# A hybrid encoder layer on one core: the embedding's squares are taken during the first gate pieces of the last stage instead of ahead of and during the down projection

## The chip, the core and the metric

The kernel runs on one core of a Trainium2 chip. A core has a matrix engine (TensorE, PE in the profile), a vector engine (VectorE, DVE), a scalar engine (ScalarE, ACT), GpSimd (POOL) and a queue that issues DMAs (SP). Each runs its own list of instructions in order; they meet at semaphores. The metric is the device time of one execution in microseconds (us), the median of several.

## The reference, cut to what matters

```python
def rmsnorm(x, g):
    y = x32 * lax.rsqrt(jnp.mean(x32 * x32, axis=-1, keepdims=True) + RMS_EPS)
    return (y * g.astype(jnp.float32)).astype(x.dtype)
...
    gu = rmsnorm(h, g_ffn[i]) @ w_gate_up[i]
    g_, u_ = gu[..., :D_FF], gu[..., D_FF:]
    h = h + (jax.nn.silu(g_) * u_) @ w_down[i]

    e = rmsnorm(p[i] @ w_ple_proj[i], g_ple_post[i])
    gate = jax.nn.sigmoid(rmsnorm(h, g_ple[i]) @ w_ple_gate[i])
    h = h + gate * e
return rmsnorm(h, g_final)
```

There are 512 tokens and 2048 model columns. Ahead of these lines come the two attention branches, which the change doesn't touch. Two norms matter here. The **residual's norm** is that of `h` after the down projection: the gate's matmul takes `h` unnormed and its result is scaled by the norm afterwards. The **embedding's norm** is that of `p @ w_ple_proj`, called `e` before it is normed.

## The kernel before, in words

Everything is held transposed: 128 columns of the model on the partitions, 512 tokens along a row, so `h` (`res`) and `e` (`emb`) are 16 tiles of 128x512 each. Float32 products are made exact by splitting each operand in a high and a low part. A **piece** of weights is 512x256: SP loads it to `raw`, ACT copies the high part (`whi`, L726, `w_hi<-raw`), DVE subtracts it for the low part (`wlo`, L1165, `w_lo<-raw,w_hi`), and PE does 24 matmuls with it (4 row tiles, 2 column tiles, 3 products: L375 to L377). There are two buffers of split weights, so ACT's split of piece n+2 waits until PE has finished piece n.

The end of the program has these stages. **E** (4 pieces, E0 to E3): the embedding's projection; DVE copies each finished pair of tiles to `emb`. **D** (8 pieces, D0 to D7): the last down projection. For each d, DVE adds the product of D<d> to the residual (`add_residual`, L1496), ACT copies the high part of the two new residual tiles times their gain (L726, `r<-res,gn`), and DVE computes their low parts (`gain_lo`, L1200). **G** (32 pieces, G0 to G31): the gate's matmul, eight groups of four pieces. The code calls the pieces `N_E + j`, `N_D + d` and `N_PLE + j`; a group of G is `g` there. The last group, with the final norm's tail, is cut in halves of the tokens.

A norm needs a sum of squares over 16 tiles. ACT squares a tile into one of two slots of `tab` (`square`, L744), POOL adds the slot to a running sum (`add_square`, L1633 for the first, a copy, and L1636 for the others), and each square waits until the slot's last sum is done. PE adds over the partitions with a matrix of ones (`total`, L399), ACT takes a logarithm and an exponential (`root`, L749 and L752), and DVE refines the result (`recip`, four instructions, L1184 to L1191). In code, `total(5, 3)` and `root(4, ...)` with `recip(4, ...)` are the residual's norm, `total(4, 2)` and `root(5, ...)` with `recip(5, ...)` the embedding's.

Before the change ACT takes the embedding's squares three at a time from E1 on (`three_squares`), 16 of the embedding, then 16 of the residual, until D's last piece. So at d = 2 to 7 the squares of residual tiles come in threes or twos, some an iteration late; at d = 6 and d = 7 two squares of new tiles stand between the residual's add and the copies with gain. Both norms are finished during G4 to G7.

In stage G, for each group, DVE scales PE's result (`empty`, L1177), ACT takes a sigmoid (L1127), DVE norms two embedding tiles (L1583, `emb<-emb,gn,rstd`), POOL multiplies the two (L1665) and adds the result to the residual (L1673), and ACT squares the new residual for the final norm and copies it with its gain (`after_gate`). The order of each engine's list is written out by hand.

Of the kernel before, what the change touches and what calls it, by code (L numbers as in the profile page):

```python
# [95 lines left out]
def build(nc, xT, pT, gains, tables, mats, w_in, w_qb, w_kvb, w_a, w_b, w_o, w_gu, w_dn, w_pg, w_pp, outT):  # L96
    with ExitStack() as ctx:
# [77 lines left out]
        def ff_pair(g):  # L175
            return (g - G_FF + 2) % 4
# [193 lines left out]
        def _(pe):  # L370
# [24 lines left out]

            def total(norm, bank):

                pe.wait_ge(acc_done, [16, 20, 24, 40, 56, 72][norm])
                mm(ps[:, bank, :], ones, sums(norm), start=True, stop=True).then_inc(tot_done, 1)  # L399

            def head_total(m):
# [229 lines left out]
            def n_group(g, n, pair):  # L631
                free(g, 4)
                for j in range(4):
                    piece(n + j, j, 2 * pair, [n_tile(4 * j + k) for k in range(4)], j == 0, j == 3)
# [45 lines left out]
                piece(N_PLE + j, j, 2 * ff_pair(G_PLE), [n_tile(4 * j + k) for k in range(4)], j == 0, j == 3)  # L680
            pe.wait_ge(emptied, G_PLE)
            total(5, 3)
            total(4, 2)
            n_group(G_PLE + 1, N_PLE + 4, ff_pair(G_PLE + 1))
            n_group(G_PLE + 2, N_PLE + 8, ff_pair(G_PLE + 2))
            pe.wait_ge(rstd_done, 6)
            n_group(G_PLE + 3, N_PLE + 12, ff_pair(G_PLE + 3))
# [36 lines left out]
        def _(act):  # L724
# [15 lines left out]
            def square(s, tile, sq, need, count):  # L740
                act.wait_ge(need, count)
                if s >= 2:
                    act.wait_ge(acc_done, s - 1)
                nc.scalar.activation(sq[:, s % 2, :], tile, ACT.Square).then_inc(sq_done, 1)  # L744
# [315 lines left out]
            def chunk(c, last):  # L1060


                b, g = c * 24 + N_FF_LOOP, c * 12 + G_FF
                four(b)
                whi(b + 6, 2)
                ff_hidden(c * 2, 0, b)
                for j in range(3):
                    whi(b + 7 + j, (3 + j) % 4)
                ff_gate(g + 2)
                four(b + 8)  # L1070
                if not last:
                    whi(b + 14, 2)
                    ff_hidden(c * 2 + 1, 1, b)
                    for j in range(3):
                        whi(b + 15 + j, (3 + j) % 4)
                    ff_gate(g + 4)
                    for d in range(8):
                        whi(b + 18 + d, (2 + d) % 4)
                else:
                    for i in range(4):  # L1080
                        whi(b + 14 + i, (2 + i) % 4)
                        if i == 0:
                            ff_hidden(c * 2 + 1, 1, b)
                        if i:
                            three_squares(i - 1)

            def three_squares(slot):

                for i in range(3 * slot, min(3 * slot + 3, 32)):
                    k, g = i % 16, (G_E if i < 16 else G_D) + i % 16 // 2  # L1090
                    square(40 + i, emb[:, k, :] if i < 16 else res[:, k, :], sq_b, emptied, g + 1)

            with act.Fori(0, CHUNKS - 1) as c:
                chunk(c, False)
# [1 line left out]
            ln_exp_table()  # L1096
            for d in range(8):
                whi(N_D + d + 2, (2 + d) % 4)
                three_squares(3 + d)
                for t in range(2):  # L1100
                    k = 2 * d + t
                    act.wait_ge(emptied, G_D + d + 1)
                    copy(n_tile(k)[:, 0, :], res[:, k, :], gn[:, G_PLEN + k:G_PLEN + k + 1]).then_inc(u_hi, 1)
# [4 lines left out]
                for k in (2 * g, 2 * g + 1):  # L1108
                    copy(emb[:, k, :], res[:, k, :], gn[:, G_FIN + k:G_FIN + k + 1]).then_inc(gained, 1)

            for g in range(8):
                b = N_PLE + 4 * g
                if g not in (1, 7):
                    whi(b + 2, 2)
                if g < 7:
                    whi(b + 3, 3)
                if g:
                    after_gate(g - 1)
                for j in range(0 if g == 7 else 4 if g == 6 else 2):
                    whi(b + 4 + j, j)  # L1120
                if g == 0:
                    root(4, 3, 2, D)
                    root(5, 2, 1, D)
                    whi(b + 6, 2)
                if g < 7:
                    act.wait_ge(emptied, G_PLE + g + 1)
                    nc.scalar.activation(tmp[:, 0:2, :], tmp[:, 0:2, :], ACT.Sigmoid).then_inc(pg_sig, 1)  # L1127
            def tail_sigmoid(th, t):
                act.wait_ge(tail_emptied, 2 * th + t + 1)
                x = tmp[:, t, HALF[th]]  # L1130
# [21 lines left out]
        def _(dve):  # L1152
# [40 lines left out]
            def recip(turn, norm, bank, r, width, t=slice(0, SEQ)):  # L1193
                refined(rstd[:, r, t], sums(norm)[:, t], ps[:, bank, t], width, log_done, root_done, turn, refine,
                        rstd_done)
                dve.wait_ge(rstd_done, turn + 1)
# [367 lines left out]
            for d in range(8):  # L1564
# [2 lines left out]
                dve.wait_ge(emptied, G_D + d + 1)  # L1567
                for k in (2 * d, 2 * d + 1):
                    gain_lo(n_tile(k), res[:, k, :], G_PLEN + k, 42 + k)
            for g in range(8):  # L1570
                for j in range(1 if g == 1 else 0, 0 if g == 7 else 6 if g == 6 else 4):
                    wlo(N_PLE + 4 * g + 2 + j, (2 + j) % 4)
                if g == 0:
                    recip(4, 5, 3, 2, D)
                if g:
                    dve.wait_ge(pg_res, g)
                if g < 7:
                    empty(tmp[:, 0:2, :], 2 * ff_pair(G_PLE + g), 2, N_PLE + 4 * g + 3)
                if g == 0:
                    wlo(N_PLE + 6, 2)  # L1580
                    recip(5, 4, 2, 1, D)
                for k in (2 * g, 2 * g + 1):
                    stt(emb[:, k, :], emb[:, k, :], gn[:, G_POST + k:G_POST + k + 1], rstd[:, 1, :],  # L1583
                        ALU.mult, ALU.mult).then_inc(emb_normed, 1)

            def tail_empty(th, t):
                dve.wait_ge(tail_tile, 2 * th + t + 1)
# [34 lines left out]
        @block.gpsimd  # L1622
        def _(pool):
            def add_square(s, first, norm, sq):

                out = sums(norm)
                pool.wait_ge(sq_done, s + 1)
                if s == first:
                    if norm == 4:
                        pool.wait_ge(u_lo, 42)  # L1630
                    elif norm:
                        pool.wait_ge(rstd_done, 4 if norm == 5 else norm)
                    nc.gpsimd.tensor_copy(out, sq[:, s % 2, :]).then_inc(acc_done, 1)  # L1633
                else:
                    pool.wait_ge(acc_done, s)
                    nc.gpsimd.tensor_tensor(out, out, sq[:, s % 2, :], ALU.add).then_inc(acc_done, 1)  # L1636

            sq_a, sq_b = tmp[:, 2:4, :], tab[:, 0:2, :]
            for norm, first, end in ((0, 0, 16), (1, 16, 20), (2, 20, 24)):
                for s in range(first, end):  # L1640
                    add_square(s, first, norm, sq_a)

            for p in range(8):
                pool.wait_ge(emptied, G_MERGE + p + 1)
                if p:
                    pool.wait_ge(mrg_lo, p)
                else:
                    pool.wait_ge(gated_a_out[0], 16 * HEADS // 2)
                nc.gpsimd.tensor_tensor(tmp[:, 0:2, :], tmp[:, 2:4, :],  # L1649
                                        res[:, GATE_IN[p % 2]:GATE_IN[p % 2] + 2, :], ALU.add).then_inc(mrg_sum, 1)  # L1650
            for s in range(24, 40):
                add_square(s, 24, 3, sq_b)
            with pool.Fori(0, CHUNKS) as c:
                for half in range(2):
                    pool.wait_ge(emptied, c * 12 + G_FF + 2 + 2 * half)
                    pool.wait_ge(ff_act, c * 2 + half + 1)
                    nc.gpsimd.tensor_tensor(tmp[:, 2:4, :], tmp[:, 2:4, :], tmp[:, 0:2, :],  # L1657
                                            ALU.mult).then_inc(ff_mul, 1)
            for norm, first in ((4, 40), (5, 56)):
                for s in range(first, first + 16):  # L1660
                    add_square(s, first, norm, sq_b)
            for g in range(7):
                pool.wait_ge(pg_sig, g + 1)
                pool.wait_ge(emb_normed, 2 * g + 2)
                nc.gpsimd.tensor_tensor(tmp[:, 0:2, :], tmp[:, 0:2, :], emb[:, 2 * g:2 * g + 2, :],  # L1665
                                        ALU.mult).then_inc(pg_mul, 1)
                pool.wait_ge(pg_mul, g + 1)
                if g == 0:
                    pool.wait_ge(u_hi, 58)
                    pool.wait_ge(u_lo, 58)  # L1670
                    pool.wait_ge(sq_done, 72)
                r = res[:, 2 * g:2 * g + 2, :]
                nc.gpsimd.tensor_tensor(r, r, tmp[:, 0:2, :], ALU.add).then_inc(pg_res, 1)  # L1673
                for s in (72 + 2 * g, 73 + 2 * g):
                    add_square(s, 72, 6, sq_b)
# [77 lines left out]
```

## Time and profile before

| what | us |
|---|---|
| median of 3 runs | 2825.78 (2824.82 to 2825.94) |
| the profiled execution's own time | 2825.82 |
| its span, first to last instruction | 2824.0 |
| PE busy | 2793.9 of 2824.0 |
| DVE, ACT, POOL busy | 1216.2, 886.5, 236.2 |
| PE waiting for DVE's low parts (L1165), whole program | 5.0, six times |

The span is 1.8 us shorter than the execution's own time; a shift of the program's end moves both alike. PE is busy in 99% of the span, so little else can matter: the other engines count only where PE waits for them, and those places are few and short.

### The profile page before, as it was taken

Reading aid. Unit: us, or ns where it says so; the run is one execution under the profiler, and the core shown is the slowest. Engines: PE = TensorE matmul, PEld = TensorE weight load, DVE = VectorE, ACT = ScalarE, POOL = GpSimd, SP = SyncE. Lnnn points to the kernel's source line nnn. Section 1 sums busy time; section 2 is a strip of 40 time slices with the busy share of each in tenths; the row PEclk is TensorE's granted clock in tenths of the full one; section 3 lists DMA queues with packets and bytes.
Section 4 is the critical chain, followed back from the end, with each engine's and each line's share of the span. In section 5 each row is a group of like instructions: output and inputs, shape, how many; then the busy total and the mean of one; then the engine's idle time right before and its main releaser. Section 6 shows DMA issues by size and latency. Waiting matters only on the chain.

```text
span 2824.0 us, 32043 instructions
## 1 busy us (share of the span) xinstructions
PE 2793.9 (99%) x12532; PEld 2305.4 (82%) x12532; DVE 1216.2 (43%) x1268; ACT 886.5 (31%) x1105; POOL 236.2 (8%) x134
## 2 busy tenths in 40 slices
PE   8999999999999999999999999999999999999998
PEld 6878888888888888888888888888888888888787
DVE  5455545455664434433333333334333333335535
ACT  5234334334554233322222222222222222224433
POOL 3000000010000211000000000000000000004332
PEclk9999999999999999999999999999999999999999
DMA  6333333333224643333333333333333333333232
GB/s 197 96 90 105 102 99 104 97 90 112 94 94 140 206 144 97 99 103 97 97 97 97 97 97 97 96 96 96 97 95 96 95 96 96 96 97 94 90 97 97
DMA packets 278895, 295.20 MB, mean 105 GB/s; under 512 B 9008, under 2 KB 261040, under 8 KB 278704
## 3 DMA queue, kind: packets, MB, share of 16 engines
q1 hardware_dynamic: 274336, 285.90, 32.6%
q10 hardware_dynamic: 4496, 8.44, 0.8%
q8 instruction: 42, 0.69, 0.1%
q14 instruction: 21, 0.17, 0.0%
HBM read 277.53 MB, written 16.78 MB: 104 GB/s over the span
## 4 chain that ended last, share of the span: by engine, by line
PE 94%; DVE 2%; POOL 2%; ACT 1%; issue 1%; DMA 0%; DVEq 0%; POOLq 0%; ACTq 0%
PE ps L375 31%; PE ps L377 31%; PE ps L376 31%; PE ps L441 1%; POOL acc L1636 1%; POOL tab L1636 1%; DVE w_lo L1165 1%; PE ps L430 0%; DVE r L1200 0%; ACT r L726 0%; PE ps L403 0%; ACT w_hi L726 0%; ACT tab L744 0%; DVE emb L1603 0%; PE ps L399 0%
## 5 line engine op out<-in xcount | busy, mean ns | idle before, releaser
L375 PE MATMUL ps<-r,w_hi 128*128 128x512 f32 x3840 | 1505.7, 392 | 13.1 <-DVE r L1200 8.1
L377 PE MATMUL ps<-r,w_lo 128*128 128x512 f32 x3840 | 1496.1, 390 | 0.0
L376 PE MATMUL ps<-r,w_hi 128*128 128x512 f32 x3840 | 1495.8, 390 | 0.0
L1165 DVE TENSOR_TENSOR w_lo<-raw,w_hi 128x1024 fp32r<-128x1024 f32 x484 | 612.1, 1265 | 1409.8 <-ACT w_hi L726 1409.0
L726 ACT ACTIVATE w_hi<-raw 128x1024 fp32r<-128x1024 f32 x484 | 512.7, 1059 | 1543.6 <-PE ps L377 1534.9
L375 PEld LDWEIGHTS ps<-r,w_hi 128*128 128x128 f32 x3840 | 721.9, 188 | 172.0 <-issue 13.0
L376 PEld LDWEIGHTS ps<-r,w_hi 128*128 128x128 f32 x3840 | 721.9, 188 | 151.7 <-issue 3.4
L377 PEld LDWEIGHTS ps<-r,w_lo 128*128 128x128 f32 x3840 | 721.7, 188 | 150.7
L1657 POOL TENSOR_TENSOR tmp<-tmp 128x1024 f32<-128x1024 f32 x22 | 52.6, 2392 | 1339.0 <-DVE tmp L1177 1339.0
L1496 DVE TENSOR_TENSOR res<-ps,res 128x1024 f32<-128x1024 f32 x96 | 116.8, 1216 | 0.0
L1177 DVE TENSOR_TENSOR tmp<-ps,rstd 128x1024 f32<-128x1024 f32 x69 | 83.9, 1217 | 1.6 <-PE ps L377 1.5
L1636 POOL TENSOR_TENSOR acc<-acc,tab 128x512 f32<-128x512 f32 x43 | 66.2, 1540 | 157.0 <-ACT tab L744 153.6
L726 ACT ACTIVATE r<-ps 128x512 fp32r<-128x512 f32 (+1 forms) x98 | 53.9, 594 | 58.9 <-PE ps L377 48.5
L375 PE MATMUL ps<-r 128*128 128x512 f32 (+1 forms) x192 | 69.6, 363 | 1.3 <-DVE r L1226 1.3
L377 PE MATMUL ps<-r 128*128 128x512 f32 (+1 forms) x192 | 68.1, 355 | 0.0
L376 PE MATMUL ps<-r 128*128 128x512 f32 (+1 forms) x192 | 68.0, 354 | 0.0
L1200 DVE SCALAR_TENSOR_TENSOR r<-res,gn,r 128x512 fp32r<-128x512 f32 x48 | 48.3, 1040 | 21.9 <-ACT r L726 21.9
L1649 POOL TENSOR_TENSOR tmp<-tmp,res 128x1024 f32<-128x1024 f32 x8 | 20.0, 2505 | 350.0 <-DVE tmp L1418 350.0
L1633 POOL COPY acc<-tmp 128x512 f32<-128x512 f32 x3 | 2.0, 683 | 546.0 <-ACT tmp L744 546.0
L1247 DVE TENSOR_TENSOR r<-ps,r 128x512 fp32r<-128x512 f32 x64 | 41.0, 681 | 7.5 <-ACT r L726 7.5
L726 ACT ACTIVATE r<-res 128x512 fp32r<-128x512 f32 (+1 forms) x39 | 24.6, 630 | 62.1 <-DVE res L1219 52.8
L726 ACT ACTIVATE r<-tmp 128x1024 fp32r<-128x1024 f32 x30 | 31.5, 1049 | 38.9 <-POOL tmp L1649 38.1
(104 smaller groups left out, 969.8 us busy)
## 6 DMA issues: line engine op xcount, KB each, us to landing
raw<-w_gu SPq DMA_DIRECT2D x176, 512.0 KB, 3.6
raw<-w_in SPq DMA_DIRECT2D x108, 512.0 KB, 3.7
raw<-w_dn SPq DMA_DIRECT2D x88, 512.0 KB, 3.4
raw<-w_o SPq DMA_DIRECT2D x32, 512.0 KB, 3.4
raw<-w_pg SPq DMA_DIRECT2D x32, 512.0 KB, 3.4
gates<-tmp ACTq DMA_DIRECT2D x16, 512.0 KB, 2.8
raw<-w_a SPq DMA_DIRECT2D x16, 512.0 KB, 3.7
res<-gates SPq DMA_DIRECT2D x16, 512.0 KB, 5.3
```

Of the source, the lines that this page charges most:

```text
L375: mm(out, hi, x[:, 0, :], start=start, stop=False)
L376: mm(out, hi, x[:, 1, :], start=False, stop=False)
L377: return mm(out, lo, x[:, 0, :], start=False, stop=stop)
L441: i = nc.tensor.transpose(ps[:, banks[kt], q * P:(q + 1) * P], res[:, PROB + q, kt * P:(kt + 1) * P], ident)
L726: return nc.scalar.activation(out, in_, ACT.Copy, scale=scale)
L1165: tt(w_lo[:, j % HL], raw[:, j], w_hi[:, j % HL], ALU.subtract).then_inc(w_lo_done, 1)
L1177: tt(out, ps[:, bank:bank + 2, :], both(r), ALU.mult).then_inc(emptied, 1)
L1200: stt(out[:, 1, :], in_, gn[:, gain:gain + 1], out[:, 0, :], ALU.mult, ALU.subtract).then_inc(u_lo, 1)
L1247: tt(pt[kt % 3][:, 1, :], ps[:, banks[kt], :], pt[kt % 3][:, 0, :], ALU.subtract).then_inc(pt_lo, 1)
L1496: tt(r, ps[:, 2 * pair:2 * pair + 2, :], r, ALU.add).then_inc(emptied, 1)
L1636: nc.gpsimd.tensor_tensor(out, out, sq[:, s % 2, :], ALU.add).then_inc(acc_done, 1)
L1657: nc.gpsimd.tensor_tensor(tmp[:, 2:4, :], tmp[:, 2:4, :], tmp[:, 0:2, :], ALU.mult).then_inc(ff_mul, 1)
```

## The change

Three things move. The squares of the residual keep their place in D, but are alone there: two for each d, right after the residual's add and ahead of the two copies with gain. The squares of the embedding go to stage G: three after the split of G2, of G3 and of G4, three more after G6's, four after G7's. And the embedding's norm follows one group later: PE's total stands after G7 instead of ahead of G4, ACT's root after the split of G9, DVE's refinement after G9's low part, and DVE norms the embedding tiles of groups 0 and 1 together there.

```diff
-                pe.wait_ge(acc_done, [16, 20, 24, 40, 56, 72][norm])
+                pe.wait_ge(acc_done, [16, 20, 24, 40, 72, 56][norm])
...
             total(5, 3)
+            n_group(G_PLE + 1, N_PLE + 4, ff_pair(G_PLE + 1))
             total(4, 2)
-            n_group(G_PLE + 1, N_PLE + 4, ff_pair(G_PLE + 1))
...
-                        if i:
-                            three_squares(i - 1)
-
-            def three_squares(slot):
-
-                for i in range(3 * slot, min(3 * slot + 3, 32)):
-                    k, g = i % 16, (G_E if i < 16 else G_D) + i % 16 // 2
-                    square(40 + i, emb[:, k, :] if i < 16 else res[:, k, :], sq_b, emptied, g + 1)
+
+            def emb_squares(k0, k1):
+
+                for k in range(k0, k1):
+                    square(56 + k, emb[:, k, :], sq_b, emptied, G_D)
...
                 whi(N_D + d + 2, (2 + d) % 4)
-                three_squares(3 + d)
+                for t in range(2):
+                    k = 2 * d + t
+                    square(40 + k, res[:, k, :], sq_b, emptied, G_D + d + 1)
...
+            for i in range(3):
+                whi(N_PLE + 2 + i, (2 + i) % 4)
+                emb_squares(3 * i, 3 * i + 3)
+            whi(N_PLE + 5, 1)
+            root(4, 3, 2, D)
+            whi(N_PLE + 6, 2)
+            ple_sigmoid(0)
+            emb_squares(9, 12)
+            whi(N_PLE + 7, 3)
+            emb_squares(12, 16)
+            whi(N_PLE + 8, 0)
+            whi(N_PLE + 9, 1)
+            root(5, 2, 1, D)
+            whi(N_PLE + 10, 2)
+            whi(N_PLE + 11, 3)
+            after_gate(0)
+            ple_sigmoid(1)
+            whi(N_PLE + 12, 0)
+            after_gate(1)
+            whi(N_PLE + 13, 1)
+            ple_sigmoid(2)
...
+            for j in range(2, 6):
+                wlo(N_PLE + j, j % 4)
+            recip(4, 5, 3, 2, D)
+            ple_empty(0)
+            for j in range(6, 10):
+                wlo(N_PLE + j, j % 4)
+            recip(5, 4, 2, 1, D)
+            emb_norm(0)
+            emb_norm(1)
+            wlo(N_PLE + 10, 2)
+            wlo(N_PLE + 11, 3)
+            ple_empty(1)
+            emb_norm(2)
+            wlo(N_PLE + 12, 0)
+            wlo(N_PLE + 13, 1)
+            ple_empty(2)
...
-            for norm, first in ((4, 40), (5, 56)):
+            for norm, first in ((5, 40), (4, 56)):
```

Line numbers shift by up to 17 in the changed kernel; the helpers are the same. The first place is ACT's list in stage D, from the split of D3 to that of D5 (`tab<-emb` and `tab<-res` are squares, `r<-res,gn` the copies with gain). Before:

```order
L726 ACTIVATE w_hi<-raw 128x1024
L744 ACTIVATE tab<-emb 128x512 x3
L726 ACTIVATE r<-res,gn 128x512 x2
L726 ACTIVATE w_hi<-raw 128x1024
L744 ACTIVATE tab<-emb 128x512
L744 ACTIVATE tab<-res 128x512 x2
L726 ACTIVATE r<-res,gn 128x512 x2
L726 ACTIVATE w_hi<-raw 128x1024
```

The same stretch in the changed kernel:

```order
L726 ACTIVATE w_hi<-raw 128x1024
L744 ACTIVATE tab<-res 128x512 x2
L726 ACTIVATE r<-res,gn 128x512 x2
L726 ACTIVATE w_hi<-raw 128x1024
L744 ACTIVATE tab<-res 128x512 x2
L726 ACTIVATE r<-res,gn 128x512 x2
L726 ACTIVATE w_hi<-raw 128x1024
```

The embedding's squares are gone, and in every iteration two squares of the tiles that the copies read next stand ahead of those copies.

The second place is ACT's list from the split of G7 to that of G11, in the changed kernel. L749 and L752 are the logarithm and the exponential of the embedding's norm; before, they stood right behind the residual's, ahead of the split of G6, with no table load between or ahead of them.

```order
L726 ACTIVATE w_hi<-raw 128x1024
L744 ACTIVATE tab<-emb 128x512 x4
L726 ACTIVATE w_hi<-raw 128x1024 x2
L749 ACT_TABLE_LOAD
L749 ACTIVATE rstd<-ps,eps 128x512
L752 ACT_TABLE_LOAD
L752 ACTIVATE rstd<-rstd 128x512
L726 ACTIVATE w_hi<-raw 128x1024 x2
```

The first sigmoid now stands ahead of this root, so two loads of ACT's function tables come with it, and a third ahead of the next sigmoid.

The third place is DVE's list from the four subtractions of G6 to G9 to those of G10 and G11, in the changed kernel (L1201 to L1208 are `recip`, L1594 the embedding's norm):

```order
L1182 TENSOR_TENSOR w_lo<-raw,w_hi 128x1024 x4
L1201 TENSOR_SCALAR tab<-ps 128x512
L1204 TENSOR_TENSOR tab<-tab,rstd 128x512
L1206 SCALAR_TENSOR_TENSOR tab<-tab,rstd 128x512
L1208 SCALAR_TENSOR_TENSOR rstd<-tab,rstd 128x512
L1594 SCALAR_TENSOR_TENSOR emb<-emb,gn,rstd 128x512 x4
L1182 TENSOR_TENSOR w_lo<-raw,w_hi 128x1024 x2
```

Before, `recip` of the embedding stood after the subtraction of G6 with two `emb` instructions behind it, and three subtractions behind those. Now it stands after G9's, with four `emb` instructions between it and G10's subtraction.

## Rows read from the trace of the kernel before

**Rows 1.** The page's first part: busy us, share of the span, instructions.

```profile
PE 2793.9 (99%) x12532; PEld 2305.4 (82%) x12532; DVE 1216.2 (43%) x1268; ACT 886.5 (31%) x1105; POOL 236.2 (8%) x134
```

**Rows 2.** Waits of PE, whole program: total us, times, longest.

```profile
PE ps L375 <- DVE w_lo L1165: 5.0, 6, 1.1
```

**Rows 3.** Timeline of PE, its late starts: start us, us, what, [idle, releaser].

```profile
2614.07 0.47 PE L375 MATMUL ps<-r,w_hi 128*128 128x512 f32 x1 [0.56 <-DVE w_lo L1165]
...
2639.55 0.47 PE L375 MATMUL ps<-r,w_hi 128*128 128x512 f32 x1 [0.90 <-DVE w_lo L1165]
...
2675.22 0.47 PE L375 MATMUL ps<-r,w_hi 128*128 128x512 f32 x1 [1.02 <-DVE w_lo L1165]
```

**Rows 4.** Timeline of ACT: splits of E2, D2, G4, G5, G6, G10.

```profile
2564.64 1.06 ACT L726 ACTIVATE w_hi<-raw 128x1024 fp32r<-128x1024 f32 x1 [4.38 <-PE ps L377]
...
2586.48 1.06 ACT L726 ACTIVATE w_hi<-raw 128x1024 fp32r<-128x1024 f32 x1
...
2645.34 1.06 ACT L726 ACTIVATE w_hi<-raw 128x1024 fp32r<-128x1024 f32 x1 [5.54 <-PE ps L377]
2650.78 1.06 ACT L726 ACTIVATE w_hi<-raw 128x1024 fp32r<-128x1024 f32 x1 [4.38 <-PE ps L377]
...
2657.98 1.06 ACT L726 ACTIVATE w_hi<-raw 128x1024 fp32r<-128x1024 f32 x1 [3.67 <-PE ps L377]
...
2681.04 1.06 ACT L726 ACTIVATE w_hi<-raw 128x1024 fp32r<-128x1024 f32 x1 [2.20 <-PE ps L377]
```

**Rows 5.** Timeline, iteration d = 7 of stage D: DVE, then ACT.

```profile
2631.56 1.21 DVE L1165 TENSOR_TENSOR w_lo<-raw,w_hi 128x1024 fp32r<-128x1024 f32 x1
2632.70 1.21 DVE L1496 TENSOR_TENSOR res<-ps,res 128x1024 f32<-128x1024 f32 x1
2635.81 2.45 DVE L1200 SCALAR_TENSOR_TENSOR r<-res,gn,r 128x512 fp32r<-128x512 f32 x2 [1.90 <-ACT r L726]
2638.19 1.21 DVE L1165 TENSOR_TENSOR w_lo<-raw,w_hi 128x1024 fp32r<-128x1024 f32 x1
...
2633.94 1.15 ACT L744 ACTIVATE tab<-res 128x512 f32<-128x512 f32 x2 [3.29 <-DVE res L1496]
2635.00 1.32 ACT L726 ACTIVATE r<-res,gn 128x512 fp32r<-128x512 f32 x2
```

**Rows 6.** Timeline of POOL and DVE where they overlap.

```profile
2609.90 1.78 DVE L1200 SCALAR_TENSOR_TENSOR r<-res,gn,r 128x512 fp32r<-128x512 f32 x1
2611.29 1.55 POOL L1636 TENSOR_TENSOR acc<-acc,tab 128x512 f32<-128x512 f32 x1
2611.61 2.31 DVE L1165 TENSOR_TENSOR w_lo<-raw,w_hi 128x1024 fp32r<-128x1024 f32 x1
...
2681.68 2.40 POOL L1673 TENSOR_TENSOR res<-res,tmp 128x1024 f32<-128x1024 f32 x1
2682.14 3.03 DVE L1165 TENSOR_TENSOR w_lo<-raw,w_hi 128x1024 fp32r<-128x1024 f32 x1 [3.06 <-ACT w_hi L726]
...
2636.09 1.62 POOL L1636 TENSOR_TENSOR acc<-acc,tab 128x512 f32<-128x512 f32 x1
2636.48 1.78 DVE L1200 SCALAR_TENSOR_TENSOR r<-res,gn,r 128x512 fp32r<-128x512 f32 x1
...
2602.13 0.61 POOL L1633 COPY acc<-tab 128x512 f32<-128x512 f32 x1
```

**Rows 7.** Timeline: ACT's table load and a root; DVE's recip and norm.

```profile
2585.18 1.28 ACT L797 ACT_TABLE_LOAD   x1
...
2651.74 0.67 ACT L749 ACTIVATE rstd<-ps,eps 128x512 f32<-128x512 f32 x1
2652.44 0.63 ACT L752 ACTIVATE rstd<-rstd 128x512 f32<-128x512 f32 x1
...
2661.01 0.69 DVE L1187 TENSOR_TENSOR tab<-tab,rstd 128x512 f32<-128x512 f32 x1
...
2663.18 1.42 DVE L1583 SCALAR_TENSOR_TENSOR emb<-emb,gn,rstd 128x512 f32<-128x512 f32 x2
```

More of the change, by code:

```diff
@@ L1109, in after_gate, with ple_sigmoid @@
                     copy(emb[:, k, :], res[:, k, :], gn[:, G_FIN + k:G_FIN + k + 1]).then_inc(gained, 1)
-            for g in range(8):
+            def ple_sigmoid(g):
+                act.wait_ge(emptied, G_PLE + g + 1)
+                nc.scalar.activation(tmp[:, 0:2, :], tmp[:, 0:2, :], ACT.Sigmoid).then_inc(pg_sig, 1)
+            for i in range(3):
[19 more added lines that the diff above has]
+            ple_sigmoid(2)
+            for g in range(3, 8):
                 b = N_PLE + 4 * g
-                if g not in (1, 7):
+                if g < 7:
                     whi(b + 2, 2)
-                if g < 7:
                     whi(b + 3, 3)
-                if g:
-                    after_gate(g - 1)
+                after_gate(g - 1)
                 for j in range(0 if g == 7 else 4 if g == 6 else 2):
                     whi(b + 4 + j, j)
[L1121 to L1124, printed above, removed]
                 if g < 7:
-                    act.wait_ge(emptied, G_PLE + g + 1)
-                    nc.scalar.activation(tmp[:, 0:2, :], tmp[:, 0:2, :], ACT.Sigmoid).then_inc(pg_sig, 1)
+                    ple_sigmoid(g)
             def tail_sigmoid(th, t):
@@ L1569, in _, with ple_empty, emb_norm @@
                     gain_lo(n_tile(k), res[:, k, :], G_PLEN + k, 42 + k)
[L1570 to L1574, printed above, removed]
+            def ple_empty(g):
                 if g:
                     dve.wait_ge(pg_res, g)
[L1577 to L1581, printed above, removed]
+                empty(tmp[:, 0:2, :], 2 * ff_pair(G_PLE + g), 2, N_PLE + 4 * g + 3)
+            def emb_norm(g):
                 for k in (2 * g, 2 * g + 1):
@@ L1584, in _ @@
                         ALU.mult, ALU.mult).then_inc(emb_normed, 1)
+            for j in range(2, 6):
[14 more added lines that the diff above has]
+            ple_empty(2)
+            for g in range(3, 8):
+                for j in range(0 if g == 7 else 6 if g == 6 else 4):
+                    wlo(N_PLE + 4 * g + 2 + j, (2 + j) % 4)
+                if g < 7:
+                    ple_empty(g)
+                else:
+                    dve.wait_ge(pg_res, 7)
+                emb_norm(g)
             def tail_empty(th, t):
```

## The prediction

> **What bounds the kernel now.** I read the page's busy shares first: PE works 99% of the span [rows 1], so a change of the other engines is worth only what it does to PE's waits. The list of PE's waits comes next: the one that repeats is for DVE's low parts, six times, 5.0 us [rows 2]. PE's timeline then says where: five late starts are in this part of the program, four between D6 and G2 (the first and the last are shown) and one at G8 [rows 3].
>
> An idle time of PE is not the whole loss, so I count in finishing times. ACT's split of piece n+2 waits for PE's end of piece n, and where ACT was idle its start is that end. Undisturbed pieces end 5.44 us apart (2645.34 to 2650.78) and the two totals together cost 2657.98 - 2650.78 - 5.44 = 1.76, so 0.88 each [rows 4]. E0 ends at 2564.64, so D0 ends four pieces later at 2586.40; ten more give 2640.80 for G2, and the row has 2645.34: stage D and the first gate pieces lose **4.54 us** [rows 4]. G7 then ends at 2645.34 + 5 x 5.44 + 1.76 = 2674.30, G8 should at 2679.74 and does at 2681.04: **1.30 us** [rows 4]. After that nothing is late until the tail. A late low part makes its piece end 5.95 us after it: G2's ends at 2638.19 + 1.21 = 2639.40, G2 itself at 2645.34 [rows 4, 5].
>
> Why is stage D late? One iteration shows it [rows 5]. DVE's chain is: subtraction at 2631.56, add at 2632.70, then it waits for ACT, which after the add makes two squares (2633.94) and only then the copies (2635.00); the two `gain_lo` start at 2635.81, the next subtraction at 2638.19. That is 6.63 us a piece against PE's 5.44. Part of the 6.63 is the second `gain_lo`, 1.78 long.
>
> **DVE and POOL exclude each other.** POOL's add started at 2611.29 while a `gain_lo` ran, DVE's next subtraction was issued at 2611.61, and they ended in the order gain, add (2612.84), subtraction (2613.92): the waiting POOL instruction went in between two DVE instructions, and the subtraction took 2.31 us for 1.21, ending 1.08 after the add. Behind a 2.40 us add on POOL a subtraction took 3.03, ending 1.09 after it; a `gain_lo` ended at 2638.26, 0.55 after the add that held it [rows 6]. DVE instructions that read a bank of sums (`res<-ps,res`) keep their 1.21 next to POOL [rows 5]. So POOL's work on 1024 elements, 2.4 us, blocks a whole low part. The Trainium skill ("SBUF — State Buffer", Who interferes with whom) has this as an exclusive lock for DVE instructions with two inputs in SBUF; by that, the trace agrees, and it speaks against putting DVE's embedding norm just ahead of a needed subtraction.
>
> **The change part by part.**
>
> Stage E: ACT loses its squares and POOL its adds. PE wasn't late there, so 0. D2's split starts at 2586.40 and not 2586.48, where a table load had held it [rows 4, 7], its subtraction at 2587.49.
>
> Stage D: the loop now has at every d the form that d = 7 had: two squares of new tiles, then the copies. I take the measured 6.63 for each, since the same instructions stand in the same order with POOL idle at the start [rows 5]. The first iteration I estimate at 6.38: there POOL's first instruction is a copy of 0.61 [rows 6] in place of an add, and by my stepping through it DVE is held 0.25 less. So G2's subtraction is issued at 2587.49 + 6.38 + 7 x 6.63 = 2640.28. Before it was 2638.19: the seven iterations from D2's subtraction (2586.48 + 1.09) to 2631.56 took 6.28 on average [rows 4, 5], less than 6.63, since most had squares of tiles that were long ready and could be made before the add. I add one collision: the first embedding square's copy on POOL is ready about 2640.0, while the last `gain_lo` runs (to 2640.35), gets in ahead of the subtraction and takes 0.47. The subtraction ends at 2640.35 + 0.47 + 1.08 = 2641.90 (2641.5 without the collision, 2643 if it were an add), G2 at 2647.85: **+2.51 us** against before.
>
> G3 to G8: one total stays ahead of G4, so G7 ends at 2647.85 + 27.20 + 0.88 = 2675.93. ACT's 16 embedding squares go at POOL's pace, an add each of 1.3 us alone and up to 1.2 more behind a DVE instruction (1.55 and 1.62 in [rows 6] after short waits). Their tightest place is behind G7's split: four squares put G8's split at about 2672.1, and its subtraction, behind POOL's last add, ends at 2675.5. With the second total ahead of G8, PE needs it by 2676.3, so G8 is in time by 0.8 and the old wait there is gone: **-1.30 us**. That wait had come from `after_gate(0)` ahead of G8's split, and this now stands behind G11's.
>
> G10: here a new wait forms. From G7's end (t = 0): split of G9 1.06; table load 1.28; logarithm 0.67; second load 1.28; exponential 0.63; with 0.02 between them the root is done at 5.00 [rows 7]. DVE's remaining three of `recip` take from their start to the first norm instruction 2663.18 - 2661.01 = 2.17 [rows 7], with 0.11 to notice: 7.28. The norm instructions follow every 0.67 [rows 7]. After two of them (8.70) POOL may start its first product, gets in after the third (9.37) and ends at 11.62 (2.40 less the 0.15 of overlap that a waiting POOL instruction shows); the fourth norm ends at 12.17; POOL's residual add waits since 11.7, ends at 14.42; only then G10's subtraction, which was issued at about 12.1, ends at 15.50. G10 so ends at 21.45, where PE would have had it at 0.88 + 3 x 5.44 = 17.20: **+4.25 us**. Behind the blocked subtraction stand G11's, `empty` of group 1 and its norm; I followed them: G12's low part is 0.8 us early, G14's 0.5, so no further wait. The DMAs don't move: SP loads a piece once the low part four pieces back is done, as before, and a low part that is 4 us late leaves it more than three pieces of 5.44 us.
>
> Bounds of the G10 term: 0 if DVE kept the port through its four norms and the subtraction (done at 11.1); about 2 if it got it back after POOL's product; 4.25 if POOL comes first both times, which is what every overlap in the trace shows, so I take that. The table loads have a row, 1.28, with the next instruction 0.02 behind (2585.18 + 1.28 to 2586.48) [rows 4, 7]. The Trainium skill ("ScalarE: Activation LUTs", What ACT_TABLE_LOAD costs) gives about 2.66 us for every switch of sets, a drain being added to the load; by it the G10 term would be 2.8 us more. The row here has no such drain.
>
> **Sum.** 2.51 - 1.30 + 4.25 = 5.46. The profiled execution took 2825.82, 0.04 above the median of the runs; 2825.82 + 5.46 = **2831.3 us**, 0.19% slower. A measurement can tell about 0.2% (5.65 us) from no change, so this forecast sits on that border.
>
> **Rivals.**
> - *Main case*, chance 0.64: 2830.3 to 2832.3, from the first iteration (0.25), the collision at G2 (-0.4 to +1) and spreads of tenths.
> - *The port goes to DVE at G10*, 0.14: the term is 0 to 2, so 2827.0 to 2829.1. For it: DVE issues back to back. Against it: rows 6.
> - *Stage D keeps PE's pace*, the faster side, 0.07. For it: POOL had three adds per piece and ACT stood waiting for POOL in most iterations; now there are two. If the iteration fell to 5.44 or below, the 4.54 would vanish: 2825.82 - 4.54 - 1.30 + 4.25 = 2824.2, and 2820.0 with the case above. Against it: the 6.63 iterations are just those where ACT did not wait for POOL, and their chain of subtraction, add, two squares, copy and two `gain_lo` is what remains. It decides at 5.44.
> - *A further low part comes late*, 0.12: the 0.8 us at G8 or the 0.5 at G14 is used up by one more collision of 1.1 to 2.4 us: 2832.5 to 2834.
> - *Each table load costs its drain too*, 0.03: 2834.1. By the rows no load does.
>
> **How the numbers follow.** The main case and the near halves of the second and fourth hold 0.8 from 2828.5 to 2833.3. Slower by over 0.2% (above 2831.4): somewhat under half of the main case, and the last two, 0.45. Faster by over 0.2% needs both the faster side and no wait at G10, or something unseen: 0.04. The rest, 0.51, is within 0.2%.
>
> **What would show it.** In the changed profile: subtractions 6.6 us apart through stage D, and PE late at D5 or D6, D7, G0, G1 and G2; no late start at G8; two table loads of 1.28 around the logarithm; POOL's 2.4 us product and add around the fourth `emb` norm, then a subtraction of over 3 us, and one idle time of PE of about 4 us at G10. I am wrong if stage D's subtractions come closer than 6.3 us apart, or if G10's subtraction ends before POOL's residual add.

## The result, and the profile after

The changed kernel took **2833.47 us** (median of 12 runs, 2831.33 to 2834.22), the kernel before 2825.86 (12 runs, 2824.82 to 2827.73): ratio 1.0027, 95% interval 1.0019 to 1.0034. It is slower by 7.6 us. That is 2.2 us more than the 2831.3 forecast, and just outside the range of 2828.5 to 2833.3.

The waits of PE in the changed kernel, whole program (total us, times, longest), answer to [rows 2]:

```profile
PE ps L375 <- DVE w_lo L1182: 9.6, 8, 3.7
```

5.0 us in six waits became 9.6 in eight, and one wait alone is 3.7. PE's timeline gives their places, for those in stages D and G, and answers to [rows 3]:

```profile
2607.80 0.47 PE L375 MATMUL ps<-r,w_hi 128*128 128x512 f32 x1 [0.33 <-DVE w_lo L1182]
2614.43 0.47 PE L375 MATMUL ps<-r,w_hi 128*128 128x512 f32 x1 [0.91 <-DVE w_lo L1182]
...
2641.36 0.47 PE L375 MATMUL ps<-r,w_hi 128*128 128x512 f32 x1 [1.34 <-DVE w_lo L1182]
2690.68 0.80 PE L375 MATMUL ps<-r,w_hi 128*128 128x512 f32 x1 [3.75 <-DVE w_lo L1182]
```

These are D5, D6 and, behind three more like D6's, G2, and then G10; G8, late before, is in time. ACT's splits of D2, G4, G9, G10 and G12, whose starts are PE's ends of D0, G2, G7, G8 and G10, answer to [rows 4]:

```profile
2585.81 1.06 ACT L726 ACTIVATE w_hi<-raw 128x1024 fp32r<-128x1024 f32 x1 [3.08 <-PE ps L377]
...
2647.14 1.06 ACT L726 ACTIVATE w_hi<-raw 128x1024 fp32r<-128x1024 f32 x1 [0.39 <-PE ps L377]
...
2675.25 1.06 ACT L726 ACTIVATE w_hi<-raw 128x1024 fp32r<-128x1024 f32 x1 [2.78 <-PE ps L377]
...
2681.60 1.06 ACT L726 ACTIVATE w_hi<-raw 128x1024 fp32r<-128x1024 f32 x1 [1.34 <-PE ps L377]
...
2699.20 1.06 ACT L726 ACTIVATE w_hi<-raw 128x1024 fp32r<-128x1024 f32 x1 [4.80 <-PE ps L377]
```

Counted as in the prediction: from D0's end ten pieces of 5.44 us lead to 2640.21, G2 ended at 2647.14, a loss of 6.93 us against 4.54 before. G7 ended when it should (2675.25), so did G8 (2681.60 = 2675.25 + 0.88 + 5.44 + 0.03). G10 should have ended at 2675.25 + 17.20 = 2692.45 and ended at 2699.20: 6.75 us lost, where 4.25 were forecast.

The timeline of DVE and then of POOL around that place:

```profile
2680.28 0.69 DVE L1204 TENSOR_TENSOR tab<-tab,rstd 128x512 f32<-128x512 f32 x1 [1.25 <-ACT rstd L752]
...
2682.47 4.88 DVE L1594 SCALAR_TENSOR_TENSOR emb<-emb,gn,rstd 128x512 f32<-128x512 f32 x4
2687.27 4.91 DVE L1182 TENSOR_TENSOR w_lo<-raw,w_hi 128x1024 fp32r<-128x1024 f32 x2
...
2684.02 2.77 POOL L1701 TENSOR_TENSOR tmp<-tmp,emb 128x1024 f32<-128x1024 f32 x1 [10.36 <-DVE emb L1594]
2686.87 2.68 POOL L1709 TENSOR_TENSOR res<-res,tmp 128x1024 f32<-128x1024 f32 x1
```

The four norm instructions take 4.88 us instead of four times 0.67, POOL's product and add lie in between and behind them, and the two low parts (merged in one row) take 4.91. All of that is as forecast, to about 0.1 us. What was not forecast is in the granted clock of TensorE. The windows of the same trace (length, then busy us and count of PE, PEld, DVE, ACT and POOL, then granted clock):

```profile
2686.00:2690.60 4.60, 0.94 (x5) 0.44 (x3) 4.60 (x3) 2.08 (x3) 3.80 (x3) 0.90 0.00 0
2690.60:2696.60 6.00, 5.92 (x14) 4.66 (x15) 4.03 (x5) 3.69 (x5) 4.69 (x3) 0.51 0.55 177
2696.60:2720.00 23.40, 23.40 (x104) 19.36 (x104) 6.38 (x5) 9.84 (x13) 14.09 (x8) 1.00 0.24 80
```

In the 6 us behind the wait the granted clock is 0.51, the lower of its two levels, 1.2 GHz. PE's rows there:

```profile
2691.28 0.63 PE L376 MATMUL ps<-r,w_hi 128*128 128x512 f32 x1
2691.70 0.63 PE L377 MATMUL ps<-r,w_lo 128*128 128x512 f32 x1
```

Matmuls start 0.43 us apart instead of 0.23.

### The profile page after: what moved, and what is told of

Same layout as the page of the kernel before. It is cut to its first block, busy times and chain, and to the rows that moved or that the text cites. A ratio compares the mean times of both kernels' runs of the same rounds, so it can differ in the third digit from the quotient of the medians.

```text
span 2831.5 us, 32046 instructions
## 1 busy us (share of the span) xinstructions
PE 2796.6 (99%) x12532; PEld 2306.6 (81%) x12532; DVE 1219.4 (43%) x1268; ACT 890.7 (31%) x1108; POOL 233.8 (8%) x134
## 4 chain that ended last, share of the span: by engine, by line
PE 94%; DVE 3%; ACT 1%; POOL 1%; issue 1%; DMA 1%; DVEq 0%; SPq 0%; ACTq 0%; POOLq 0%
PE ps L375 31%; PE ps L377 31%; PE ps L376 30%; PE ps L441 1%; DVE r L1217 1%; DVE w_lo L1182 1%; POOL acc L1672 1%; PE ps L430 0%; DMA raw<-w_o 0%; ACT r L726 0%; DVE res L1513 0%; ACT w_hi L726 0%; PE ps L403 0%; DVE emb L1639 0%; ACT tab L744 0%
```

## The experiments

Each edit is to the changed kernel, unless another is named; the kernel before ran beside them, at 2825.73, 2825.99 and 2826.47 us in three sessions. Runs 1 to 4 were of one session, 5 to 8 of the next, 9 of the last. Medians are of 11 runs, in run 7 of 5. The changed kernel was not run again in these sessions, so "less than the changed kernel" compares with its 2833.47 us of the session before, where the kernel before took 2825.86.

**1. DVE norms group 1 later.** In DVE's list:

```diff
             emb_norm(0)
-            emb_norm(1)
             wlo(N_PLE + 10, 2)
             wlo(N_PLE + 11, 3)
+            emb_norm(1)
             ple_empty(1)
```

> The changed kernel with one edit: DVE norms the embedding tiles of group 1 behind the low part of G11 and not ahead of that of G10. Theory A (port and clock): G10's low part is issued after two norm instructions, before POOL's first product can start, so PE's idle of 3.75 us at G10 goes, and with it the 14 matmuls that ran at 0.43 us apart behind it; together 4.25 + 2.6 = 6.9 us, so about 2826.6 us against 2833.5. Theory B (the slow matmuls have another cause than PE's idle): the idle goes, the 0.43 us spacing stays somewhere, gain 4.2 us, 2829.3. Theory C (POOL's port isn't what held the low part, the late root is): G10's low part stays late by over 2 us, gain under 2 us.

Measured: 2830.86 us (2829.53 to 2831.14), ratio to the kernel before 1.0018 (1.0009 to 1.0027); 2.6 us less than the changed kernel and not 6.9. Its timeline of DVE, then POOL, and PE's late starts of that stretch:

```profile
2682.51 1.42 DVE L1594 SCALAR_TENSOR_TENSOR emb<-emb,gn,rstd 128x512 f32<-128x512 f32 x2
2683.84 1.22 DVE L1182 TENSOR_TENSOR w_lo<-raw,w_hi 128x1024 fp32r<-128x1024 f32 x1
2688.17 2.70 DVE L1182 TENSOR_TENSOR w_lo<-raw,w_hi 128x1024 fp32r<-128x1024 f32 x1 [3.11 <-ACT w_hi L726]
...
2696.81 2.57 DVE L1182 TENSOR_TENSOR w_lo<-raw,w_hi 128x1024 fp32r<-128x1024 f32 x1 [0.76 <-ACT w_hi L726]
...
2684.07 3.24 POOL L1701 TENSOR_TENSOR tmp<-tmp,emb 128x1024 f32<-128x1024 f32 x1 [10.36 <-DVE emb L1594]
2687.39 2.40 POOL L1709 TENSOR_TENSOR res<-res,tmp 128x1024 f32<-128x1024 f32 x1
...
2695.90 2.40 POOL L1701 TENSOR_TENSOR tmp<-tmp,emb 128x1024 f32<-128x1024 f32 x1 [2.86 <-ACT tmp L1112]
...
2699.53 0.47 PE L375 MATMUL ps<-r,w_hi 128*128 128x512 f32 x1 [1.67 <-DVE w_lo L1182]
2706.31 0.50 PE L375 MATMUL ps<-r,w_hi 128*128 128x512 f32 x1 [1.08 <-DVE w_lo L1182]
```

G10's low part (2683.84) now gets in ahead of POOL's product and runs its bare 1.22 us; the wait there is gone, as theories A and B say, and the low clock with it, as A alone says. But G11's low part and the norm of group 1 meet POOL's add instead, the sigmoid behind them comes late, and with it ACT's split of G12: PE waits 1.67 and 1.08 us at G12 and G13. The clock stays at 1.00 behind these. So of this expectation only what happens at G10 was right; what queues behind it was not followed, and the time was 4.3 us over theory A's.

**2. Copies ahead of the squares in stage D.** In ACT's list:

```diff
                 for t in range(2):
                     k = 2 * d + t
-                    square(40 + k, res[:, k, :], sq_b, emptied, G_D + d + 1)
+                    act.wait_ge(emptied, G_D + d + 1)
+                    copy(n_tile(k)[:, 0, :], res[:, k, :], gn[...]).then_inc(u_hi, 1)
                 for t in range(2):
                     k = 2 * d + t
-                    act.wait_ge(emptied, G_D + d + 1)
-                    copy(n_tile(k)[:, 0, :], res[:, k, :], gn[...]).then_inc(u_hi, 1)
+                    square(40 + k, res[:, k, :], sq_b, emptied, G_D + d + 1)
```

> The changed kernel with one edit: in stage D, ACT makes the two copies with gain ahead of the two squares. Theory A (the chain add, two squares, copy is what makes 6.63 us an iteration): gain_lo starts 1.05 us earlier and its second one is no longer held by POOL, the iteration falls to about 5.7 us, which the slack at D2 (3 us) carries through eight iterations, no late start of PE up to G2: 7 us less, about 2826.4 us. Theory B (POOL's adds hold DVE wherever they fall, the order on ACT doesn't matter): the iteration stays at 6.2 us or more, as the subtraction is held in place of gain_lo, 2831 us or more.

Measured: 2827.37 us (2826.80 to 2828.25), ratio 1.0007 (0.9998 to 1.0016), 6.1 less than the changed kernel. One iteration on DVE, which answers to [rows 5]:

```profile
2600.05 1.23 DVE L1182 TENSOR_TENSOR w_lo<-raw,w_hi 128x1024 fp32r<-128x1024 f32 x1 [1.12 <-ACT w_hi L726]
2601.20 1.22 DVE L1513 TENSOR_TENSOR res<-ps,res 128x1024 f32<-128x1024 f32 x1
2603.27 1.42 DVE L1217 SCALAR_TENSOR_TENSOR r<-res,gn,r 128x512 fp32r<-128x512 f32 x2 [0.86 <-ACT r L726]
2605.81 1.23 DVE L1182 TENSOR_TENSOR w_lo<-raw,w_hi 128x1024 fp32r<-128x1024 f32 x1 [1.12 <-ACT w_hi L726]
```

5.76 us a piece, and the two `gain_lo` together take 1.42 and not 2.46. Theory A holds. Counted in finishing times, D0's end to G7's loses 0.94 us in this trace, against 6.96 in the changed kernel's, so 6.0 less. What stays are small late starts from G1 to G3 and after, since 5.76 is more than 5.44 and, at G3, since POOL's adds hold the subtraction. The idle at G10 is the same, 3.74 us, but only five of PE's starts behind it are 0.42 or 0.43 us apart, twelve in the changed kernel's trace. That makes G7's end to G10's 1.35 us shorter in this execution. It is not an effect of the edit that any other run shows.

**3. PE's idle filled.** In PE's list, ahead of G10:

```diff
+                if j == 2:
+                    pe.wait_ge(rstd_done, 5)
+                    for i in range(16):
+                        mm(ps[:, 3, :], n_tile(0)[:, 0, 0:P], n_tile(0)[:, 1, :], start=True, stop=True)
```

> The changed kernel with PE's idle at G10 filled: 16 extra matmuls of 128x512 into a bank that nothing reads afterwards stand ahead of G10's, 16 x 0.227 = 3.6 us, in an idle of 3.75 us. The low part comes no earlier. Theory A (the clock falls because PE stood idle): the matmuls of G10 are 0.227 us apart, PE's delay at G10 shrinks from 6.9 to 4.2 us, about 2830.9 us. Theory B (the slow matmuls behind the idle have to do with something else at that place): they stay 0.43 us apart, 2833.5 us.

Measured: 2831.35 us (2829.74 to 2831.86), ratio 1.0018 (1.0009 to 1.0028), 2.1 less than the changed kernel. PE's timeline and two windows of this trace:

```profile
2687.49 3.79 PE L690 MATMUL ps<-r 128*128 128x512 f32 x16
...
2691.79 0.40 PE L376 MATMUL ps<-r,w_hi 128*128 128x512 f32 x1
...
2686.00:2691.00 5.00, 5.00 (x24) 4.03 (x22) 5.00 (x2) 1.72 (x3) 4.23 (x2) 1.00 0.00 0
2691.00:2697.00 6.00, 5.82 (x26) 4.60 (x25) 4.40 (x5) 4.07 (x5) 4.66 (x3) 1.00 0.56 174
```

The low part is no earlier, the clock stays at 1.00, and PE does 26 matmuls in the 6 us in which the changed kernel had records of 14. Theory A holds: the low clock follows PE's idle, and costs 2.1 us in the medians. In finishing times it is 2.6: G10 ends 21.34 us after G7 here (2675.96 to 2697.30) and 23.95 after it in the changed kernel (2675.25 to 2699.20).

**4. One table load.** `ln_exp_table()` stands ahead of `root(5, ...)`.

> The changed kernel with the table that holds both functions loaded once ahead of the embedding's root, so that no load stands between logarithm and exponential. PE's idle at G10 should shrink by one load, 1.28 us, to about 2.45. If the clock falls behind an idle of that length too: 1.3 us less, 2832.2 us. If it doesn't: 3.9 us less, 2829.6 us.

Measured: 2831.36 us (2828.72 to 2833.53), ratio 1.0020 (1.0011 to 1.0030), 2.1 less. The longest wait of PE fell to 2.6 us and the clock fell behind it all the same; its windows:

```profile
2685.90:2688.70 2.80, 0.25 (x2) 0.00 (x0) 2.80 (x2) 2.09 (x3) 2.08 (x2) 0.95 0.00 0
2688.70:2694.00 5.30, 5.23 (x17) 4.21 (x18) 4.03 (x5) 3.69 (x5) 3.99 (x3) 0.71 0.66 194
```

The load accounts for 1.1 of the wait. In this trace G10 loses 4.37 us in place of 6.75; the other 1.3 of the difference are a shorter slow stretch (clock 0.71 over 5.3 us against 0.51 over 6). Run 2's stretch was as short behind 3.74 us, so no run shows that the shorter idle shortened it, and this kernel's runs are spread over 4.8 us.

**5. Both edits of order** (1 and 2).

> The changed kernel with both edits of order together: in stage D the copies with gain ahead of the squares, and DVE's norm of group 1 behind the low part of G11. Alone they gave 2827.37 and 2830.86 us against 2833.47 of the changed kernel, 6.1 and 2.6 less. If the two places are independent: 8.7 less, 2824.8 us, with stage D at 5.76 us an iteration and late starts at G12 and G13 as with the second edit alone. If PE, which comes earlier through the first edit, meets the same late low parts (those that hang on DVE's and POOL's chain and not on PE), less than 8.7 is saved.

Measured: 2824.80 us (2823.92 to 2826.06), ratio 0.9995 (0.9986 to 1.0004): the sum of the two, closer than runs spread over 2.1 us can resolve. The idle times at G12 and G13 are 1.65 and 1.06 us, as in run 1, so the two places don't touch.

**6. POOL's adds cut short in stage D.** `add_square` of the residual's norm copies one column in place of adding 512, so the residual's sum of squares is incomplete.

> The changed kernel with POOL's 15 additions of residual squares in stage D cut to one column each (128x1 in place of 128x512), so that the residual's sum of squares is incomplete; ACT's squares and all orders stay. It tells how much of the 6.63 us iteration is POOL's hold of the port. Theory A (half the excess over the chain is the port): the second gain_lo takes 0.75 in place of 1.79, the iteration is 5.6 us, no late start through G2, 2826.4 us. Theory B (only ACT's two squares in the chain count): 6.6 us, 2833.5 us.

Measured: 2826.37 us (2825.58 to 2827.39), ratio 1.0002 (0.9993 to 1.0011). On DVE, with both squares still ahead of the copies:

```profile
2610.09 1.22 DVE L1182 TENSOR_TENSOR w_lo<-raw,w_hi 128x1024 fp32r<-128x1024 f32 x1
2611.23 1.22 DVE L1513 TENSOR_TENSOR res<-ps,res 128x1024 f32<-128x1024 f32 x1
2614.35 1.42 DVE L1217 SCALAR_TENSOR_TENSOR r<-res,gn,r 128x512 fp32r<-128x512 f32 x2 [1.90 <-ACT r L726]
2615.84 1.23 DVE L1182 TENSOR_TENSOR w_lo<-raw,w_hi 128x1024 fp32r<-128x1024 f32 x1
```

5.75 us a piece, and D0's end to G7's loses 0.03 us in place of 6.96. Theory A holds. The 6.63 are thus 5.44 of PE's pace, plus 0.3 of pure chain, plus 0.9 of POOL's hold. The wait at G10 is still 3.75 us here.

**7. The kernel before, copies first.** The same swap in the kernel before, where three squares stand in each iteration.

> The kernel before, with ACT's two copies with gain ahead of the three squares in stage D. Theory A (the order alone is what counts, with three squares too): the late starts at D6 to G2, 4.5 us, fall under 2 us, 2823 to 2824. Theory B (three squares at POOL's pace, 4.3 us alone and more behind DVE, now stand between the copies and the next split): the iteration is 6.3 us or more, no gain, 2826 us or more. This would say that fewer squares an iteration, as in the change, is worth something once the order is right.

Measured: 2840.25 us (2839.54 to 2842.54), ratio 1.0052 (1.0038 to 1.0065): 14 us slower. ACT's timeline of one iteration:

```profile
2597.74 1.34 ACT L726 ACTIVATE r<-res,gn 128x512 fp32r<-128x512 f32 x2 [3.44 <-DVE res L1496]
2598.99 1.14 ACT L744 ACTIVATE tab<-emb 128x512 f32<-128x512 f32 x2
2601.23 0.63 ACT L744 ACTIVATE tab<-emb 128x512 f32<-128x512 f32 x1 [1.10 <-POOL tab L1636]
2601.77 1.04 ACT L726 ACTIVATE w_hi<-raw 128x1024 fp32r<-128x1024 f32 x1
...
2606.23 1.34 ACT L726 ACTIVATE r<-res,gn 128x512 fp32r<-128x512 f32 x2 [3.42 <-DVE res L1496]
```

8.5 us from one pair of copies to the next, since the third square waits for POOL ahead of the next split. The subtraction behind that split is then held by POOL's third add (2.24 us at 2594.33 for 1.23 alone). The granted clock fell behind several of PE's waits here, of 2.0 to 2.8 us, and its mean from 2596 to 2656 us is 0.91. Most of that is hidden, because PE waits for the next low part anyway; behind the last wait it isn't: G1 ends 7.59 us after its low part, not 5.95, so 1.6 of the 14 us are the clock's. Theory B, and stronger than expected: with three squares an iteration this order is bad, with two (run 2) it is good. With two squares and the copies first (run 2) D0's end to G7's loses 0.9 us, in the kernel before 4.5: that is what the sparser squares can be worth, and the change's order threw it away.

**8. Squares of tiles that are long there.** The kernel before, its squares respread; PE's and DVE's lists are untouched. `old_squares(first, end)` takes the squares first to end - 1 in the old order, 16 of the embedding and then 16 of the residual.

```diff
                         if i:
-                            three_squares(i - 1)
+                            old_squares(4 * i - 4, 4 * i)
...
                 whi(N_D + d + 2, (2 + d) % 4)
-                three_squares(3 + d)
+                old_squares(12 if d == 0 else 13 + 2 * d, 15 + 2 * d)
...
+                if g == 0:
+                    old_squares(29, 32)
...
+                if g == 1:
+                    whi(b + 4, 0)
                 if g:
                     after_gate(g - 1)
```

> The kernel before, with its squares spread anew: four of the embedding in each of the three slots of stage E, three at d = 0, and then two an iteration of tiles that are already there, the last three behind the split of G2; and the split of G8 ahead of after_gate(0). The embedding's norm stays ahead of G4. If squares of old tiles fit beside DVE's subtraction and add, and two adds of POOL an iteration leave DVE at or under 5.44 us, no start of PE is late from D0 to G8: 5.8 us less than before, 2820.0 us. If POOL's adds still land on gain_lo or the subtraction, 1 to 3 us of that stay.

Measured: 2822.42 us (2821.05 to 2823.54), ratio 0.9988 (0.9979 to 0.9997), 3.6 us below the kernel before and 2.4 over the 2820.0 expected. DVE's iterations:

```profile
2607.68 1.21 DVE L1169 TENSOR_TENSOR w_lo<-raw,w_hi 128x1024 fp32r<-128x1024 f32 x1
2608.82 1.21 DVE L1500 TENSOR_TENSOR res<-ps,res 128x1024 f32<-128x1024 f32 x1
2610.89 1.82 DVE L1204 SCALAR_TENSOR_TENSOR r<-res,gn,r 128x512 fp32r<-128x512 f32 x2 [0.86 <-ACT r L726]
2612.63 1.21 DVE L1169 TENSOR_TENSOR w_lo<-raw,w_hi 128x1024 fp32r<-128x1024 f32 x1
```

4.95 us, under PE's 5.44, and G8 is in time. What stayed late is D2 and D3, with 0.15 and 1.55 us of idle and 2.24 us in finishing times up to G2 (the expectation of run 9 puts them at 0.3 and 1.7). The cause would be the four squares a slot in stage E, which held the split of D2 until 2589.64, and the three at d = 0; run 9 takes both away.

**9. The same, with three in stage E and two throughout stage D**, the last seven behind the splits of G2 and G3. Against run 8:

```diff
-                            old_squares(4 * i - 4, 4 * i)
+                            old_squares(3 * i - 3, 3 * i)
...
-                old_squares(12 if d == 0 else 13 + 2 * d, 15 + 2 * d)
+                old_squares(9 + 2 * d, 11 + 2 * d)
...
-                    old_squares(29, 32)
+                    old_squares(25, 28)
...
+                if g == 0:
+                    old_squares(28, 32)
```

> As the kernel before this (squares of tiles that are long there), but stage E keeps its three squares a slot, as in the kernel before the change, stage D has two at every d from d = 0 on, and the last seven stand behind the splits of G2 (three) and G3 (four). The two late starts that were left, 0.3 us at D2 and 1.7 us at D3, came from four squares a slot in stage E, which held the split of D2 back by 3 us, and from three at d = 0. If that is so, no start of PE is late from D0 to G8, and the time is 2 us below 2822.4: 2820.2 us, 5.8 below the kernel before. If the seven squares behind D's end hold back the splits of G3 to G5 instead, a late start of 1 us or more appears there.

Measured: **2820.74 us** (2819.34 to 2821.88), ratio 0.9980 (0.9971 to 0.9989), 5.7 us below the kernel before. No start of PE is late between D0 and the tail; its wait for low parts is down to one early in the program:

```profile
PE ps L375 <- DVE w_lo L1171: 0.5, 1, 0.5
```

Both losses of the kernel before are gone, 4.54 us from D0's end to G7's and 1.30 at G8, 5.84 together. The first goes with the squares; the second with G8's split, which now stands ahead of `after_gate(0)`.

## Why the prediction was wrong, point by point

**What bounds the kernel** held, and so did the way of counting: losses of PE at single pieces, taken from ACT's splits, add up to the difference. 6.93 - 4.54 = 2.39, less 1.30 at G8, plus 6.75 at G10 makes 7.84; the medians differ by 7.6. That the two agree so well is partly luck: ahead of E2 the changed execution is 0.59 us early (its split starts at 2564.05, not 2564.64), which the change can't have caused (of the two traces only that of the kernel before has a slow stretch behind its first norm, see below), and the rest of the program adds 0.3.

**Stage D**: forecast +2.51, measured +2.39. Iterations of 6.63 us from d = 1 on, a shorter first one, the late starts at D5 to G2. Run 6 shows the share of POOL's hold. Run 2 doesn't separate chain from hold: it brings the copies 1.05 us forward and also frees the second `gain_lo`, and its iteration ends in another wait, 1.12 us for ACT's split. One reading cites a row that can't show it: that `res<-ps,res` keeps its 1.21 us beside POOL is not in [rows 5], where POOL was idle at 2632.70; the add at 2596.01 in the same trace shows it, 1.21 us long beside POOL's adds of 2593.50 to 2598.68.

**The collision at G2**: forecast, the subtraction to end 1.62 us after its issue; the row in the changed profile (2639.59, G2's low part) says 1.63.

**G8**: forecast -1.30 and no late start; so it was.

**G10**: this is the step that failed, and in its second half, where a late low part was priced at 5.95 us to the end of its piece. "G10 so ends at 21.45, where PE would have had it at 17.20: +4.25 us". The late low part was right: it ended at 2690.63, 15.38 us after G7 against 15.50 forecast, PE stood idle 3.75 us, and from there 5.95 would have made 21.33. PE took 8.57 instead of 5.95 us to finish the piece, because the term took a late piece's 5.95 us from starts that were one microsecond late, at a granted clock of 1.00. After the idle of 3.75 us it was 0.51 for about 6 us. That is 2.62 us in the profiled execution, and 2.1 between the medians of the changed kernel and run 3. Run 3 shows the cause: with PE kept busy and nothing else changed there, G10 ended 21.34 us after G7, which is the 21.33 above.

That the first half was right isn't only the number: the four norms took 4.88 us for 4 x 0.67, 2.2 more, and the subtraction 3.36 (2687.27 to 2690.63) for 1.22, 2.1 more. Without these 4.3 us the low part would have been there at about 2686.3, ahead of PE's stop at 2686.93. This is an estimate from the rows; no run takes POOL's product and add away at G10.

The trace of before held a warning. Early in the program, up to 44.77 us, PE waits 1.9 us for the sum of the first norm; the windows around it show what follows, and below them stand the same wait and a window behind it in the changed kernel:

```profile
30.00:44.70 14.70, 12.83 (x57) 10.30 (x55) 4.70 (x3) 7.79 (x11) 13.33 (x10) 1.00 0.26 72
44.70:50.00 5.30, 5.24 (x14) 3.65 (x15) 5.09 (x7) 1.32 (x2) 0.00 (x0) 0.68 0.57 170
...
45.54 1.10 PE L399 MATMUL ps<-acc,cm 128*128 128x512 f32 x2 [2.03 <-POOL acc L1672]
...
45.50:50.80 5.30, 5.26 (x21) 3.79 (x22) 5.09 (x7) 1.32 (x2) 0.00 (x0) 1.00 0.56 156
```

In the kernel before, the granted clock was 0.68 in the 5.3 us behind that idle. In the changed kernel it stayed at 1.00 behind 2.03 us of idle at the same place, which the change doesn't touch. Of the eleven traces kept here it fell there in four (the kernel before, runs 2, 5 and 8, waits of 1.94 to 2.17 us) and not in seven (1.80 to 2.06 us). So the place tells that a slow stretch may follow a wait, and neither that it will nor how long it lasts. A forecast that opened an idle of 4 us should have carried it as a rival: half speed over a similar stretch, 5.3 x (1 - 0.68) = 1.7 us and up, puts 2831.3 at 2833 or more, and would have widened the range.

**The table loads** cost 1.28 us each with the next instruction 0.01 to 0.02 behind (2676.33 to 2677.62 in the changed trace), so the rival of a drain at each load falls:

```profile
2676.33 1.28 ACT L749 ACT_TABLE_LOAD   x1
2677.62 0.69 ACT L749 ACTIVATE rstd<-ps,eps 128x512 f32<-128x512 f32 x1
```

**The other rivals**: POOL came first at the port both times, so the case in which DVE keeps it fell. Stage D did not keep PE's pace. No further low part was late in the changed kernel. In run 1, where PE is not late at G10, G12 and G13 were; DVE's order differs there too, so it doesn't test the 0.8 us that the prediction gave G12.

## What to carry to other kernels

Where one engine is busy 99% of the time, add up its lateness piece by piece, and price every idle that an edit opens twice: the wait itself, and the slow stretch that may follow it; look for idle times elsewhere in the trace and read the granted clock behind them, in several executions if there are, since one can show a fall where the next shows none. Work that two engines can't do at once (here DVE's low parts and POOL's adds) is cheap only where neither is waited for. Squares of tiles that are long there fit in the gaps of ACT's list; squares of the tile just made lengthen the chain, and moving a norm later puts its whole refinement, its table loads and its consumers in front of a deadline.

## What the runs showed of the hardware that was not expected

- TensorE's granted clock fell behind idles of 3.75 us (changed kernel, 0.51 over the next 6 us) and 2.6 us (run 4, 0.71 over 5.3 us), and stayed at 1.00 behind 1.67 us (run 1) and where no idle was left (run 3). Behind about 2 us it did either: 0.68 behind 1.94 us in the kernel before, 1.00 behind 2.03 us at the same place in the changed kernel. How long it stayed low differed too: behind 3.75 us twelve of PE's starts were 0.42 or 0.43 us apart in the changed kernel, behind 3.74 us five in run 2. Why is open.
- In the first 4 us of PE's work the windows give a granted clock of 1.00, but the matmuls from 8.66 to 11.65 us of the kernel before are 0.43 us apart, as at the lower level elsewhere. There the spacing tells more than the column.
- A POOL instruction that waited for the port got it between two DVE instructions that stood back to back, at G2 and twice at G10 in the changed kernel, as in [rows 6].
